# Two 64-row halves of experts side by side in TensorE's column groups, and the tail in token rows, in a hybrid encoder step on one core

## The chip, the cores and the metric

One Trainium2 chip, one of its cores. The metric is the device time of one execution in microseconds, the median of several runs; lower is better. Everything is float32.

## What is computed

One layer of a streaming encoder for 1024 prompt tokens and 8 sequences of 16 sample tokens, 1152 tokens of width 1024: RMSNorm, four mixer branches with gates, an output projection, then a second RMSNorm and a mixture of 16 experts, then a final RMSNorm. The change touches the experts and what is behind them:

```python
def _layer(...):
    ...
    h = _rmsnorm(x, P['norm_moe_w']) * (1.0 + sc_f) + sh_f
    f = _grouped_moe(h.reshape(bsz * L, D_MODEL), router_w, router_bias, ...)
    x = x + g_f * f.reshape(bsz, L, D_MODEL)

def _grouped_moe(h, router_w, router_bias, w_gate, w_up, w_down):
    ...
    def expert_block(args):
        xb, e = args
        return (jax.nn.silu(xb @ w_gate[e]) * (xb @ w_up[e])) @ w_down[e]
    yb = lax.map(expert_block, (buf.reshape(...), block_expert)).reshape(...)
    return jnp.zeros_like(h).at[t_s].add(yb[pos] * w_s[:, None])
```

The router picks two experts for every token, with weights. The width inside an expert is 512. g_f is one vector for all prompt tokens and one for each sample sequence. The 1152 tokens make 2304 rows, sorted by expert. On the reference's own inputs its router gives the 16 experts 102, 183, 150, 119, 126, 153, 182, 129, 163, 195, 169, 191, 79, 120, 128 and 115 rows. In blocks of 128 rows these fill 25 of the kernel's 33 blocks; in halves of 64 rows they fill 42 of 52. Blocks and halves behind the last one are given to expert 15 and computed too, since the program is the same for any routing.

## The kernel before

Five engines run their own instruction streams (blocks `nc.sync` or SP, which issues nearly all DMAs; `nc.tensor` or PE; `nc.scalar` or ACT; `nc.gpsimd` or POOL; `nc.vector` or DVE), each in the order written, and meet at hand-written semaphores.

The router's result goes through a stretch of small operations on DVE with transposes and small matmuls on PE, which gives for each block its expert and the token of each row. The normed tokens have been written to DRAM as rows (`h_rows`). Then come the blocks, 0 to 32. POOL gathers 128 rows into `xg`; PE turns them (`turn_block`, L1260, 8 transposes), ACT copies them to `xT`. PE multiplies them by the gate weights and by the up weights (L1291, 8 + 8 matmuls of 512 columns into banks 0 and 1), ACT and DVE form silu(gate) * up, PE turns that (L1301, 4 transposes), and multiplies it by the down weights (`down_block`, L1277, 8 matmuls). PE's order in block j is gate, up, turn of block j + 1, down of block j - 1, turn of the hidden rows of j.

An expert's weights are 6 MB: 2 MB gate, 2 MB up, 2 MB down. SBUF has room for two sets, and the blocks use them in turn by expert: the address comes from a register. SP's loop reads three numbers for block j from a table (`value_load`: expert of the next set, whether block j begins a new expert, and the address of the other set), and when block j begins a new expert it loads the expert after it into the other set (L826 gate and up, L829 down). An issue with `cond` false moves nothing. Then SP stores the output rows of block j - 1 to DRAM (L709).

The tail is three phases with barriers between them (`end_phase`). For each of 9 chunks of 128 tokens POOL gathers the two output rows of a token (L1683), DVE scales and adds them (L2239, L2240), PE turns the sum to feature layout (L1312), DVE multiplies by g_f (L2246) and adds x (L2250). Then the final RMSNorm over all tokens (squares on ACT, sums with a matrix of ones on PE, L510; the root on ACT; the reciprocal and the scaling on DVE, L530 and L2254), then one store of the whole output and three small ones.

## Time and profile before

| what | value |
|---|---|
| median of 3 runs | 3228.3 us (3225.89 to 3230.79) |
| the profiled execution, its time | 3229.76 us |
| its span, first to last instruction | 3227.6 us |
| mean granted TensorE clock | 0.943 |
| busy: PE, PEld, DVE, ACT, POOL | 2881.0, 1727.9, 1119.8, 673.8, 48.8 us |
| busy on L1291 (gate, up) and L1277 (down) | 461.5 and 232.2 us |

PE is the matmul stream and PEld the loading of its stationary operand, which runs beside it. A float32 matmul of the program is two MATMUL records in the trace, a transpose is one. Starts are what counts: the end of a record is modelled, and records of a full stream overlap. The granted clock is 1.0 for 2.4 GHz and 0.5 for 1.2 GHz. SPq is SP's queue of DMA issues.

### The profile page before, as it was taken

The numbers are of one execution on the slowest core, as the hardware profiler recorded it, in microseconds if no ns is written. First come the engines' busy times: TensorE is split into PE (matmuls) and PEld (weight loads), VectorE is DVE, ScalarE is ACT, GpSimd is POOL, SyncE is SP. The second block draws the span as 40 slices with busy tenths as digits, with TensorE's granted clock in tenths as the row PEclk, the third lists the DMA queues.
The fourth block names the chain that finished last, engine by engine and source line by source line (L and its number), as shares of the span: only waits on it lengthen the run. The fifth ranks groups of instructions, "written<-read, shape, count | busy, mean of one in ns | idle before, by whom it ended". The sixth has DMA issues, their size and how long they took to land. (4 is left out here: it accounts for less than half of the span.)

```text
span 3227.6 us, 27447 instructions
## 1 busy us (share of the span) xinstructions
PE 2881.0 (89%) x10827; PEld 1727.9 (54%) x10827; DVE 1119.8 (35%) x1718; ACT 673.8 (21%) x1144; POOL 48.8 (2%) x56
## 2 busy tenths in 40 slices
PE   6998999989899997898599998989879999999953
PEld 3556777765455665454355566655434444444422
DVE  5794444324232354331311567223430000000034
ACT  2442322212111111112200265311301011011001
POOL 0000000000000000000000000000000000000010
PEclk9999999979999998999799999999979999999976
DMA  6001121112010112110001101230165745573132
GB/s 260 27 26 58 41 89 65 37 37 111 26 52 26 41 49 107 56 53 26 26 26 39 40 24 48 96 134 6 59 257 192 271 172 196 202 278 133 40 107 95
DMA packets 41260, 292.73 MB, mean 91 GB/s; under 512 B 4528, under 2 KB 17200, under 8 KB 29872
## 3 DMA queue, kind: packets, MB, share of 16 engines
q1 hardware_dynamic: 33792, 264.24, 21.0%
q0 software_dynamic: 7344, 26.74, 2.5%
q8 instruction: 89, 1.46, 0.2%
q14 instruction: 35, 0.29, 0.0%
HBM read 345.52 MB, written 46.11 MB: 121 GB/s over the span
## 5 line engine op out<-in xcount | busy, mean ns | idle before, releaser
L492 PE MATMUL psum<-arena 128*128 128x384 f32 x3168 | 1037.7, 490 | 80.4 <-DVEq L318 61.8
L492 PEld LDWEIGHTS psum<-arena 128*128 128x128 f32 x3168 | 606.8, 192 | 509.1 <-DVEq L318 65.5
L1291 PE MATMUL psum<-arena 128*128 x1056 | 461.5, 595 | 1.9 <-ACT arena L1640 1.9
L652 PE MATMUL psum<-arena 128*128 128x384 f32 x1152 | 406.6, 497 | 16.8 <-DMA arena<-in_gate 14.3
L1291 PEld LDWEIGHTS psum<-arena 128*128 128x128 f32 x1056 | 199.1, 191 | 241.0 <-issue 241.0
L652 PEld LDWEIGHTS psum<-arena 128*128 128x128 f32 x1152 | 213.3, 194 | 138.1 <-DMA arena<-in_gate 15.2
L1277 PE MATMUL psum<-arena 128*128 x528 | 232.2, 592 | 1.1 <-DVE arena L2230 1.1
L2226 DVE TENSOR_TENSOR arena<-arena,psum 128x512 f32<-128x512 f32 x33 | 22.7, 688 | 437.3 <-issue 401.1
L1277 PEld LDWEIGHTS psum<-arena 128*128 128x128 f32 x528 | 97.8, 190 | 112.3 <-issue 112.3
L633 DVE TENSOR_TENSOR arena<-arena,psum 128x1152 f32<-128x1152 f32 x32 | 43.3, 1354 | 313.4 <-PE psum L492 313.4
L1176 PE MATMUL psum<-arena 128*128 128x384 f32 x384 | 127.8, 492 | 8.2 <-DMA arena<-in_out 8.2
L530 DVE RECIPROCAL arena<-arena 128x1152 f32<-128x1152 f32 x14 | 102.9, 7353 | 59.6 <-ACT arena L525 38.9
L1176 PEld LDWEIGHTS psum<-arena 128*128 128x128 f32 x384 | 72.9, 192 | 58.8 <-issue 11.4
L2220 DVE COPY arena<-psum 128x512 f32<-128x512 f32 x33 | 22.8, 691 | 230.4 <-PE psum L1277 230.4
L588 DVE SCALAR_TENSOR_TENSOR arena<-arena,vec 128x1024 f32<-128x1024 f32 x72 | 92.5, 1285 | 2.5
L1794 DVE TENSOR_TENSOR arena<-arena,psum 128x256 f32<-128x256 f32 x120 | 48.2, 421 | 120.9 <-PE psum L943 120.7
L931 PE MATMUL psum<-arena 128*128 128x128 f32 x480 | 76.0, 284 | 15.8 <-DVE arena L1794 12.0
L1640 ACT ACTIVATE arena<-psum 128x1024 f32<-128x1024 f32 x33 | 33.8, 1023 | 266.0 <-PE psum L1260 266.0
L557 ACT ACTIVATE arena<-hist 128x24 f32<-128x24 f32 x24 | 5.4, 226 | 349.7 <-PE psum L492 326.2
L931 PEld LDWEIGHTS psum<-arena 128*128 128x128 f32 x480 | 62.2, 191 | 29.0 <-issue 20.3
L665 ACT ACTIVATE arena<-psum 128x384 f32<-128x384 f32 x72 | 35.1, 490 | 200.1 <-PE psum L652 199.8
L510 PE MATMUL psum<-arena,cst 128*128 128x384 f32 x144 | 55.2, 536 | 23.7 <-ACT arena L518 23.7
(482 smaller groups left out, 2664.9 us busy)
## 6 DMA issues: line engine op xcount, KB each, us to landing
arena<-in_moe SPq DMA_DIRECT2D x33, 4096.0 KB
arena<-in_moe SPq DMA_DIRECT2D x33, 2048.0 KB
arena<-in_ada SPq DMA_DIRECT2D x12, 2048.0 KB, 9.0
y_rows<-arena SPq DMA_DIRECT2D x33, 512.0 KB, 2.9
arena<-in_gate SPq DMA_DIRECT2D x8, 2048.0 KB, 7.9
gate_raw<-arena SPq DMA_DIRECT2D x72, 192.0 KB, 1.8
arena<-gate_raw SPq DMA_DIRECT2D x6, 2304.0 KB, 9.2
arena<-in_br SPq DMA_DIRECT2D x4, 2048.0 KB, 9.7
```

The source lines that it names most:

```text
L492: last = nc.tensor.matmul(pset(s)[:, n, :], w[:, kk, :], src[:, kk, n * N3:(n + 1) * N3], start=(kk == 0), stop=(kk == K - 1))
L510: last = nc.tensor.matmul(pset(s)[:, n, :], ones, sq[q % 2][:, n * N3:(n + 1) * N3], start=(i == 0), stop=(i == len(terms) - 1))
L530: V.then(nc.vector.reciprocal(rs, rt), s_recip)
L588: nc.vector.scalar_tensor_tensor(out=dst[:, 0:NP_TOK], in0=a, scalar=w, in1=dst[:, 0:NP_TOK], op0=ALU.mult, op1=ALU.add)
L633: nc.vector.tensor_tensor(tri3(dst), tri3(sig), pset(s), ALU.mult).then_inc(s_free[s], 1)
L652: last = nc.tensor.matmul(bank(6 + u % 2)[:, 0:N3], w[:, m % 4, kk, :], HT[:, kk, n * N3:(n + 1) * N3], start=(kk == 0), stop=(kk == KD - 1))
L665: nc.scalar.activation(stage[k][u % 2], bank(6 + u % 2)[:, 0:N3], ACT.Copy).then_inc(g_ev, 1)
L931: last = nc.tensor.matmul(bank(5 * f)[:, hs[e]], cLK[lv % 2][:, hs[h]], gX[h], start=True, stop=True)
L1176: last = nc.tensor.matmul(bank(u % 4)[:, 0:N3], wo[m // 4][:, m % 4, k, :], merged[:, k, n * N3:(n + 1) * N3], start=(k == 0), stop=(k == ...
L1277: last = nc.tensor.matmul(bank(6 + n), ehT[:, k * P:(k + 1) * P], arena[:, bass.ds(at + (8192 + 1024 * k + 512 * n), 512)], start=(k == 0) ...
L1291: last = nc.tensor.matmul(bank(w), x[:, k * P:(k + 1) * P], arena[:, bass.ds(at + (4096 * w + 512 * k), 512)], start=(k == 0), stop=(k == ...
L1794: tt(x, x, bank(1 + f)[:, 0:256], ALU.subtract).then_inc(c_x, 1)
```

## The change

Experts. The unit is a half of 64 rows. The 52 halves stand in two lists of 26, and step j takes half j and half 26 + j: both are gathered as one tile of 128 rows. List i has a weight set of its own at a fixed address (`wset[i]`), and each matmul of before is now two, for 64 rows each, with the outputs in partitions 0 to 63 and 64 to 127 of one bank. There are 26 steps in place of 33 blocks. Since a list has one set, its three parts are overwritten in place: SP's loop waits until gate, up and down are through with the old weights and loads the new ones part by part (`load_part`), 2 MB each and each conditional. ACT now copies all 1024 columns of the result (`yr`), DVE multiplies them by the prompt's g_f (`yb`), and both are stored, to `y_raw` and `y_rows`.

Routing. The tables are fewer and the copying of g_f to rows is new: 10 small DMAs, one PE transpose. x is turned to token rows in place: 18 units of 4 transposes on PE (`x_rows`) and a copy on ACT, put between PE's waits for the routing.

Tail. It runs in token rows, without barriers between its parts: per chunk 4 gathered buffers ahead, two scaled additions on DVE, square with sum, root, reciprocal of 128 numbers, and the turn to feature layout as 8 matmuls with a diagonal matrix that holds the reciprocals, then scaled copies by half on DVE and on ACT, and a store for each chunk. The sample chunk takes its rows from `y_raw` and multiplies by its g_f. The three small output stores move ahead of the experts.

```diff
 KM = MIX // P
 GH, SH = 4, 8
 NE = 16
-BLK = 128
-NB = (2 * T + NE * (BLK - 1)) // BLK
+BLK = 64
+NBP = ((2 * T + NE * (BLK - 1)) // BLK + 1) // 2
+NB = 2 * NBP
 EPS = 1e-6
...
-        wset = cut(0, 12288)
+        wset = [cut(0, 12288), cut(WSET, 12288)]
...
+        yr = [cut(19968, D), cut(20992, D)]
+        gate_p, gate_s = cut(43520, D), cut(44544, D)
+        gate_t = cut(45568, P)[0:72]
+        yg = [[cut(WSET * (i >= 6) + 2048 * (i % 6) + 1024 * k, D) for k in range(2)] for i in range(NT)]
+        fdg = [cut(12288 + P * i, P) for i in range(2)]
+        fss, frt, frs = [small[:, 256 + 9 * i:256 + 9 * (i + 1)] for i in range(3)]
+        y_raw = nc.dram_tensor("y_raw", (NB * BLK, D), F32, kind="Internal").ap()
+        gate_rows = nc.dram_tensor("gate_rows", (72, P), F32, kind="Internal").ap()
...
         def store_block(sp, j):
 
             sp.wait_ge(e_ya, j + 1)
+            sp.dma_start(y_raw[j * P:(j + 1) * P, :], yr[j % 2]).then_inc(e_st[j % 2], 16)
             sp.wait_ge(e_yd, j + 1)
-            sp.dma_start(y_rows[j * BLK:(j + 1) * BLK, :], yb[j % 2]).then_inc(e_st[j % 2], 16)
+            sp.dma_start(y_rows[j * P:(j + 1) * P, :], yb[j % 2]).then_inc(e_st[j % 2], 16)
 
 
         @block.sync
...
+            def half_expert(j, i):
+
+                e = sp.value_load(eint[:, 0, NBP * i + j:NBP * i + j + 1], min_val=0, max_val=NE - 1)
+                return A["moe"][bass.ds(e, 1)].rearrange("a p c -> (a p) c")
+
+            first = [half_expert(0, i) for i in range(2)]
+            for i in range(2):
+                sp.dma_start(wset[i][:, 0:4096], first[i][:, 0:4096]).then_inc(e_wg, 16)
+            for i in range(2):
+                sp.dma_start(wset[i][:, 4096:8192], first[i][:, 4096:8192]).then_inc(e_wu, 16)
...
+            def load_part(j, a, b, done):
+
+                for i in range(2):
+                    new = sp.value_load(eint[:, 1, NBP * i + j:NBP * i + j + 1], min_val=0, max_val=1)
+                    sp.dma_start(wset[i][:, a:b], half_expert(j, i)[:, a:b], cond=(new > 0)).then_inc(done, 16)
+
+            for j in range(1, NBP + 1):
+                if j < NBP:
+                    sp.wait_ge(e_g, j)
+                    load_part(j, 0, 4096, e_wg)
                     sp.wait_ge(e_u, j)
-                sp.dma_start(arena[:, bass.ds(other, 8192)], expert[:, 0:8192], cond=(new > 0)).then_inc(e_w[j % 2], 16)
-                if j:
+                    load_part(j, 4096, 8192, e_wu)
                     sp.wait_ge(e_d, j)
-                sp.dma_start(arena[:, bass.ds(other + 8192, 4096)], expert[:, 8192:12288],
-                             cond=(new > 0)).then_inc(e_wd[j % 2], 16)
-                if j:
...
+                    load_part(j, 8192, 12288, e_wd)
+                store_block(sp, j - 1)
+            for s, c in enumerate(CHUNKS):
+                sp.wait_ge(f_e, s + 1)
+                sp.wait_ge(f_w, s + 1)
+                sp.dma_start(A["yT"][:, :, c * P:(c + 1) * P], hd(yg[s][1], 8)).then_inc(s_out, 16)
+            sp.wait_ge(s_out, 16 * (3 + NT))
...
+            def x_rows(v0, v1):
+
+                for v in range(v0, v1):
+                    c, u = v // 2, 2 * NT + 1 + v
+                    pe.wait_ge(m_htok, u - 1)
+                    for k in range(4):
+                        last = nc.tensor.transpose(bank(5 + u % 2)[:, P * k:P * (k + 1)],
+                                                   X[:, 4 * (v % 2) + k, c * P:(c + 1) * P], ident)
+                    last.then_inc(m_ht, 1)
...
+            def down_block(j):
+
+                pe.wait_ge(e_wd, 32 * (j + 1))
                 pe.wait_ge(e_htc, j + 1)
                 if j:
                     pe.wait_ge(e_ya, j)
-                    pe.wait_ge(e_yd, j)
                 for n in range(2):
                     for k in range(4):
-                        last = nc.tensor.matmul(bank(6 + n), ehT[:, k * P:(k + 1) * P],
-                                                arena[:, bass.ds(at + (8192 + 1024 * k + 512 * n), 512)],
-                                                start=(k == 0), stop=(k == 3))
+                        for i in range(2):
+                            o = 64 * i
+                            last = nc.tensor.matmul(bank(6 + n)[o:o + 64], ehT[:, k * P + o:k * P + o + 64],
+                                                    wset[i][:, 8192 + 1024 * k + 512 * n:8192 + 1024 * k + 512 * (n + 1)],
+                                                    start=(k == 0), stop=(k == 3))
                 last.then_inc(e_d, 1)
 
             turn_block(0)
...
+            for j in range(NBP):
                 pe.wait_ge(e_xc, j + 1)
                 x = xT[j % 2]
-                for w, s in ((0, e_g), (1, e_u)):
+                for w, ready, s in ((0, e_wg, e_g), (1, e_wu, e_u)):
+                    pe.wait_ge(ready, 32 * (j + 1))
                     for k in range(KD):
-                        last = nc.tensor.matmul(bank(w), x[:, k * P:(k + 1) * P],
-                                                arena[:, bass.ds(at + (4096 * w + 512 * k), 512)],
-                                                start=(k == 0), stop=(k == KD - 1))
+                        for i in range(2):
+                            o = 64 * i
+                            last = nc.tensor.matmul(bank(w)[o:o + 64], x[:, k * P + o:k * P + o + 64],
+                                                    wset[i][:, 4096 * w + 512 * k:4096 * w + 512 * (k + 1)],
+                                                    start=(k == 0), stop=(k == KD - 1))
                     last.then_inc(s, 1)
...
-                    down_block(j - 1, before)
+                    down_block(j - 1)
...
+            down_block(NBP - 1)
+            for s in range(NT):
+                pe.wait_ge(f_d, s + 1)
+                if s >= 4:
+                    pe.wait_ge(f_e, s - 3)
+                    pe.wait_ge(f_w, s - 3)
                 for k in range(KD):
-                    last = nc.tensor.transpose(bank(2 * (c % 2) + k // 4)[:, P * (k % 4):P * (k % 4 + 1)],
-                                               ff[c % 2][:, k * P:(k + 1) * P], ident)
+                    last = nc.tensor.matmul(bank(2 * (s % 4) + k // 4)[:, P * (k % 4):P * (k % 4 + 1)],
+                                            yg[s][0][:, k * P:(k + 1) * P], fdg[s % 2], start=True, stop=True)
                 last.then_inc(f_t, 1)
...
                 if j >= 2:
-                    act.wait_ge(e_st[j % 2], 16 * (j // 2))
-                nc.scalar.activation(yb[j % 2][:, 0:512], bank(6), ACT.Copy).then_inc(e_ya, 1)
+                    act.wait_ge(e_st[j % 2], 32 * (j // 2))
+                nc.scalar.activation(yr[j % 2], psum[:, 3072:4096], ACT.Copy).then_inc(e_ya, 1)
...
+            for s in range(NT + 2):
+                if 1 <= s < NT + 1:
+                    i = s - 1
+                    act.wait_ge(o_rs, UP_RS + i + 1)
+                    if i >= 2:
+                        act.wait_ge(f_t, i - 1)
+                    nc.scalar.activation(fdg[i % 2], ident, ACT.Identity, scale=frs[:, i:i + 1]).then_inc(f_d, 1)
+                if s >= 2:
+                    i = s - 2
+                    act.wait_ge(f_t, i + 1)
+                    for k in range(4, KD):
...
+                if s < NT:
+                    act.wait_ge(f_f, s + 1)
+                    S.then(nc.scalar.activation(yg[s][1], yg[s][0], ACT.Square, accum_out=fss[:, s:s + 1]))
+                    nc.scalar.activation(frt[:, s:s + 1], fss[:, s:s + 1], ACT.Sqrt, bias=c_("eps"),
+                                         scale=1.0 / D).then_inc(o_root, 1)
...
+            for i in range(2):
+                pool.wait_ge(e_st[i], 32 * ((NBP + 1 - i) // 2))
+            for s, c in enumerate(CHUNKS):
+                if s >= 4:
+                    pool.wait_ge(f_f, s - 3)
                 for k in range(2):
-                    pool.indirect_dma_start(out=yg[c % 2][k], out_offset=None, in_=y_rows,
+                    pool.indirect_dma_start(out=yg[s][k], out_offset=None, in_=y_raw if c == NT - 1 else y_rows,
                                             in_offset=bass.IndirectOffsetOnAxis(
-                                                ap=posi[:, NT * k + c:NT * k + c + 1], axis=0)).then_inc(f_y[c % 2], 16)
+                                                ap=posi[:, NT * k + c:NT * k + c + 1], axis=0)).then_inc(f_y[s % 4], 16)
...
+            dve_down(NBP - 1)
+            for s in range(NT + 2):
+                if s < NT:
+                    c = CHUNKS[s]
+                    y0, y1 = yg[s]
+                    xc = X[:, :, c * P:(c + 1) * P]
+                    dve.wait_ge(f_y[s % 4], 32 * (s // 4 + 1))
+                    if c < NT - 1:
+                        V.then(stt(out=hd(y0, 8), in0=hd(y0, 8), scalar=w12[:, 0, c:c + 1], in1=xc, op0=ALU.mult, op1=ALU.add))
+                    else:
+                        V.then(ts(y0, y0, w12[:, 0, c:c + 1], None, ALU.mult))
+                if 1 <= s < NT + 1:
+                    i = s - 1
+                    dve.wait_ge(o_root, UP_ROOT + i + 1)
+                    V.then(nc.vector.reciprocal(frs[:, i:i + 1], frt[:, i:i + 1]), o_rs)
+                if s < NT:
+                    if c < NT - 1:
+                        V.then(stt(out=y0, in0=y1, scalar=w12[:, 1, c:c + 1], in1=y0, op0=ALU.mult, op1=ALU.add), f_f)
+                    else:
+                        V.then(stt(out=y0, in0=y1, scalar=w12[:, 1, c:c + 1], in1=y0, op0=ALU.mult, op1=ALU.add))
+                        V.then(tt(y0, y0, gate_s, ALU.mult))
+                        V.then(tt(hd(y0, 8), hd(y0, 8), xc, ALU.add), f_f)
+                if s >= 2:
+                    i = s - 2
+                    dve.wait_ge(f_t, i + 1)
+                    tt(hd(yg[i][1][:, 0:512], 4), hd(bank(2 * (i % 4)), 4), over(v_("norm_final", 0, 4), P),
```

In the diff of the DVE part the copy of the result becomes:

```diff
             def dve_down(j):
-                dve.wait_ge(e_d, j + 1)
-                if j >= 2:
-                    dve.wait_ge(e_st[j % 2], 16 * (j // 2))
-                nc.vector.tensor_copy(yb[j % 2][:, 512:1024], bank(7)).then_inc(e_yd, 1)
-            for j in range(NB):
+                dve.wait_ge(e_ya, j + 1)
+                tt(yb[j % 2], yr[j % 2], gate_p, ALU.mult).then_inc(e_yd, 1)
+            dve.wait_ge(m_grow, 16 * (2 + NSEQ))
+            for j in range(NBP):
                 dve.wait_ge(e_sg, j + 1)
                 dve.wait_ge(e_u, j + 1)
```

What the change does to the order on SP, in the steady part of the loop. Before, from the wait for down (`e_d`) to the next gate and up load, whose weights are for a later expert:

```order
L829 ISA [waits e_d]
L829 REGISTER_ALU
L829 DMA arena<-in_moe 128x4096
L709 DMA y_rows<-arena 128x1024 [waits e_yd,e_ya]
L820 TENSOR_LOAD hist
L820 ISA x2
L821 TENSOR_LOAD hist
L821 ISA x2
L822 TENSOR_LOAD hist
L822 ISA x2
L826 ISA [waits e_u]
L826 REGISTER_ALU
```

Now, from the second set's part of down to the first set's part of gate of the next step. Ahead of these rows stands the same group of six for the first set, which begins with the wait for `e_d`; behind them stands the group of the second set's gate part:

```order
L846 TENSOR_LOAD hist
L846 ISA x2
L823 TENSOR_LOAD hist
L823 ISA x2
L847 ISA
L847 DMA arena<-in_moe 128x4096
L710 DMA y_raw<-arena 128x1024 [waits e_ya]
L712 DMA y_rows<-arena 128x1024 [waits e_yd]
L846 TENSOR_LOAD hist [waits e_g]
L846 ISA x2
L823 TENSOR_LOAD hist
L823 ISA x2
```

One load with three numbers ahead of it has become two loads with two numbers each, and the gate part that the next step reads now stands behind the wait for down and behind both stores.

On PE, a step now. The rows of L1327 are gate and up, L1299 the turn of the next rows, L1313 down of the step before, L1337 the turn of the hidden rows:

```order
L1327 MATMUL psum<-arena 64x512 [waits e_wg,e_xc]
L1327 MATMUL psum<-arena 64x512 x15
L1327 MATMUL psum<-arena 64x512 [waits e_wu]
L1327 MATMUL psum<-arena 64x512 x15
L1299 MATMUL psum<-cst,arena 128x128 [waits e_xc,e_x1]
L1299 MATMUL psum<-cst,arena 128x128 x7
L1313 MATMUL psum<-arena 64x512 [waits e_ya,e_htc,e_wd]
L1313 MATMUL psum<-arena 64x512 x15
L1337 MATMUL psum<-cst,arena 128x128 [waits e_hid]
L1337 MATMUL psum<-cst,arena 128x128 x3
```

Gate and up have a wait for their own weights (`e_wg`, `e_wu`) in every step, each count of which comes from SP's row L847 of that same step, and there are twice as many matmuls of half the rows.

## Rows read from the trace of the kernel before

**Rows 1.** The page's first line.

```profile
span 3227.6 us, 27447 instructions
```

**Rows 2.** Blocks and tail: stretch, length, busy PE, PEld, DVE, ACT, POOL, clock, DMA.

```profile
2371.90:3102.90 731.00, 727.92 (x1980) 342.86 (x1980) 64.63 (x98) 73.86 (x99) 29.03 (x31) 0.99 0.48 184
3102.90:3227.60 124.70, 35.37 (x120) 24.09 (x120) 59.77 (x46) 12.29 (x11) 16.85 (x18) 0.59 0.34 122
```

**Rows 3.** Timeline of PE and ACT in the last blocks: start, length, line.

```profile
3065.29 1.04 PE L1260 MATMUL psum<-cst,arena 128*128 128x128 f32 x8
3066.16 7.03 PE L1277 MATMUL psum<-arena 128*128 x16
3066.36 1.02 ACT L1640 ACTIVATE arena<-psum 128x1024 f32<-128x1024 f32 x1 [7.14 <-PE psum L1260]
3073.03 0.60 PE L1301 MATMUL psum<-cst,arena 128*128 128x128 f32 x4
3073.47 13.90 PE L1291 MATMUL psum<-arena 128*128 x32
3087.21 7.03 PE L1277 MATMUL psum<-arena 128*128 x16
```

**Rows 4.** Timeline of PE where 64-column operands alternate between partition halves.

```profile
1090.03 0.44 PE L1055 MATMUL psum<-arena 128*64 128x128 f32 x4
1090.25 0.44 PE L1057 MATMUL psum<-arena 128*64 128x128 f32 x4
1091.12 0.44 PE L1057 MATMUL psum<-arena 128*64 128x128 f32 x4
1091.49 1.13 PE L1071 MATMUL psum<-arena 128*128 128x256 f32 x4
```

**Rows 5.** Timeline of SP's issues in two blocks, then the L821 loads' durations.

```profile
2481.86 0.09 SPq L829 DMA_DIRECT2D arena<-in_moe  x1
2482.30 0.35 SPq L709 DMA_DIRECT2D y_rows<-arena  x1
2485.34 0.35 SPq L826 DMA_DIRECT2D arena<-in_moe  x1
...
2504.23 0.36 SPq L709 DMA_DIRECT2D y_rows<-arena  x1
2506.72 0.34 SPq L826 DMA_DIRECT2D arena<-in_moe  x1
...
L821 SPq TENSOR_LOAD <-hist x32: 261/290/855, 2370.4 to 3053.1; - x32
```

**Rows 6.** A 2 MB load alone (to landing), and 6 MB of expert weights.

```profile
arena<-in_gate SPq DMA_DIRECT2D x8, 2048.0 KB, 7.9
...
2352.39:2369.84 17.45, 7.86 (x36) 7.75 (x36) 11.95 (x29) 0.00 (x0) 2.50 (x2) 0.50 0.92 368
```

**Rows 7.** An idle stretch of PE, and stretches right behind idle ones.

```profile
257.40:266.20 8.80, 0.05 (x2) 0.04 (x1) 5.75 (x10) 3.69 (x6) 0.00 (x0) 0.70 0.63 238
266.20:274.50 8.30, 8.30 (x39) 8.30 (x40) 2.86 (x6) 2.51 (x4) 0.00 (x0) 0.50 0.00 1
1774.10:1779.80 5.70, 5.70 (x9) 3.16 (x10) 4.62 (x26) 0.19 (x2) 0.00 (x0) 0.50 0.62 267
1847.00:1851.50 4.50, 4.48 (x7) 2.52 (x8) 0.00 (x0) 4.44 (x12) 0.00 (x0) 0.50 0.00 0
2169.30:2172.30 3.00, 2.98 (x5) 1.79 (x6) 0.00 (x0) 0.00 (x0) 0.00 (x0) 0.50 1.06 401
```

**Rows 8.** The tail: costliest groups of PE and DVE, then two rows of its timeline.

```profile
L1312 PE MATMUL psum<-cst,arena 128*128 128x128 f32 x72 | 17.7, 427 | 50.8 <-DVE arena L2240 50.8
L2240 DVE SCALAR_TENSOR_TENSOR arena<-arena,hist 128x1024 f32<-128x1024 f32 x9 | 11.6, 1284 | 0.3
...
3106.58 0.94 POOL L1683 DMA_INDIRECT arena<-y_rows,hist  x1 [82.87 <-ACTq L318]
3113.38 0.75 DVE L2239 TENSOR_SCALAR arena<-arena,hist 128x1024 f32<-128x1024 f32 x1 [9.76 <-DMA arena<-y_rows,hist]
```

203 lines of the change are left out of this document (71 added, 132 removed).

## The prediction

> **What bounds the kernel now.** I read the stretches first, then the timeline of PE, then that of SP. The span is 3227.6 us [rows 1]. The change leaves everything before the router alone, so two stretches matter: the expert blocks, 731.0 us, in which PE is busy for 727.9, and the tail, 124.7 us, in which PE is busy for 35.4 and DVE for 59.8 [rows 2]. In the blocks the reader is to see a chain of PE work without a hole: turn 0.87 us (3065.29 to 3066.16), down 6.87 (to 3073.03), turn of the hidden rows 0.44 (to 3073.47), gate and up 13.74 (to 3087.21), 21.92 together [rows 3]. Weights never hold it up, since they come for the next expert, into the other set. The tail is bound by waits between engines, not by any of them.
>
> **Streams side by side.** The new step has twice the matmuls of half the rows. What two of them cost together is shown by four-record groups whose results go in turn to partitions 0 to 63 and 64 to 127: they start 0.22 us apart (1090.03, 1090.25), 0.055 for a record of 128 columns [rows 4], where 8 records one after the other take 0.87, 0.109 each [rows 3]. So two column groups run at once and a pair costs one. I take 13.74 and 6.87 us for the pairs. Going back to the full form, the next record starts 0.37 after the last group (1091.12 to 1091.49) in place of 0.22 [rows 4]: 0.15 a switch, four in a step, 0.6 (bounds 0 and 0.6). A step of pure PE work is then 21.92 + 0.6 = 22.5 us, and 26 in place of 33 would save about 140. A rule of the Trainium skill speaks against the full pairing: TensorE: Matmul & The Clock Gate, Measured speedup vs the span model, gives 2.38 times for three column tiles of 512 columns, which is 0.79 of the ideal. By it a pair would cost 1.26 of one, 5.4 us more in a step and some 140 us more in all; the trace has 1.98 times for two.
>
> **The wait that is put in.** This is the large term. Gate of step j + 1 needs `e_wg`, whose count is given by SP in every step, whether it loads or not, and these issues now stand behind the wait for down of step j - 1, behind the down parts and behind both stores. PE has only the turn of the hidden rows left when down ends. I count from there. SP's 13 instructions before (three register loads of three instructions, three for the address, of which the order doesn't print a move, and the issue) take 3.04 us less the store's 0.35 in one block and 2.49 less 0.36 in the other, plus 0.09 for an issue that moves nothing: 2.78 and 2.22, mean 2.5 [rows 5]. That two values exist is seen in L821, 0.26 to 0.86 us for the same load. A set's part now is 9 such instructions (two register loads, address, move, issue): 2.5 x 9/13 = 1.73. Four of them (down and gate, two sets each) are 6.9; the two stores are 0.44 each (2481.86 to 2482.30) [rows 5], 0.9; for the semaphores at both ends I take 0.2. Sum 8.0 us, bounds 7.2 (all loads short) and 9.0 (all long). Whether an issue that moves nothing raises its semaphore at once no row says: at least 0, at most the 7.9 of a real 2 MB load [rows 6]; I take 0, as no packet is sent. The copy on ACT (1.02 [rows 3]) and the multiplication on DVE (at most 1.28 [rows 8]) end 2.5 us after down and lie beside the down parts; without that cover they would add 2.5. Of the 8.0, 0.4 is covered by the turn of the hidden rows, so a steady step is 22.5 - 0.4 + 8.0 = 30.1 us. In the first step SP is not yet behind down, so 24 of the 25 transitions have it. Queued behind the wait on PE is all the rest of the step, and the loads of up follow gate's at once, covered by gate's 6.9 us.
>
> **The clock.** PE now stands idle some 7.5 us in each step. Before, an idle stretch of 8.80 us had a clock of 0.70 in the mean, and the work right behind was at 0.5 for 8.3 us; behind three others it was 5.7, 4.5 and 3.0 us [rows 7]. Work at 1.2 GHz loses half its time: 4.1, 2.9, 2.2, 1.5. I take 2.5 a step (bounds 1.5 and 4.1).
>
> **Loads that move something.** They are in place, so their whole length shows. The router's counts make 42 halves: list 0 changes its expert at steps 2, 5, 8, 10, 12, 15, 18, 21, 24, list 1 at 2, 5, 8, 10, 12, 14. So five steps load both sets, five load one. 2 MB take 7.9 us from issue to landing, and 6 MB 17.45 (370 GB/s), so 4.8 for each further 2 MB [rows 6]. The first issue comes 1.5 us after the stores. Both sets: 1.5 + 7.9 + 4.8 = 14.2, less the 3.5 which the two parts take anyway, 10.7 us more. One set: 9.4 - 3.5 = 5.9, or 7.6 where it is the second. Up's 2 MB parts land 4.8 apart behind gate's, within gate's 6.9 plus the slow clock. Down's have a whole step. Together 5 x 10.7 + 4 x 5.9 + 7.6, and 4 for the issues of real down parts: 89 us (bounds 60, if they overlap the steady wait better, and 120, with the gathers in the same queues).
>
> **Sum of the expert stretch.** From its start: 3.3 to the first gate; the first step 13.7 + 0.9 + 0.4, 1 for the silu, 2.5 clock, 18.5; 24 transitions of 30.1 + 2.5 = 32.6, 782; the last step and its own down 13.7 + 6.9 + 0.4 + 1.1 + 6.9 + 0.6, 29.6; loads 89. 923 us in place of 731.0, 192 more.
>
> **Routing stretch.** 18 units of 4 transposes enter PE's waits for DVE. Eight transposes take 0.87 [rows 3], so they cost 8 us, 16 at 1.2 GHz, if that cover were gone. DVE has less to compute, SP ten small DMAs more, ahead of a table that it needs only after the first gate. I take 0, bounds -3 and +5.
>
> **Tail.** Up to the first gather 5.4 us: copy 1.0, multiplication 1.3, store and its landing 3.1 as now (before 3.7 in all). First gather to DVE 6.8 (3106.58 to 3113.38) [rows 8]. Then per chunk DVE has two 1.28 [rows 8], about 0.6 for half a copy and 0.3 for the rest, 3.5; PE has 16 records in place of 8 that took 1.97 at the low clock (17.7/9) [rows 8], 3.9 at most. 9 chunks by 3.5 to 3.9 and 2 for the sample chunk: 35. Drain of the pipeline and the last store: 11. Sum 58 in place of 124.7. What goes is the 50.8 us of PE waits on L2240 and the final norm's three passes. I take -65, bounds -50 and -72.
>
> **Sum.** 192 - 65 = +127 us on a profiled execution of 3227.6 (its time was 3229.76, the median of the runs 3228.3, 1.5 lower). On the median this gives 3355; as the real loads may hide a little of the clock's loss (the ten longest waits have one ramp, too) I round down to 3350.
>
> **Rivals.**
> - *SP's chain is short* (faster side). If a part costs 0.8 us and not 1.73, the chain is 4.3 us, the idle time under 4, and the clock may stay up: 24 x (3.7 + 2.5) = 149 less, 3201. The chain decides below about 5 us, if the clock holds with it. For it speaks the 0.09 us of an idle issue; against it both rows of SP, where three loads never took under 2 us. Chance 0.05.
> - *Pairs overlap only in part.* 512 columns in two groups may not stream as 128 do. If a pair costs a quarter more than one: 26 x 5.2 = 134 more, 3484; with no overlap at all 26 x 20.6 more, 3886. Against it stands [rows 4]. The 1.26 of the Trainium skill (TensorE: Matmul & The Clock Gate, as above) would give 3490. Chance 0.05.
> - *The loads cost more than I count*: weights, gathers and two stores in the same queues, up parts late too, so that each of the ten load steps costs 8 us more and the steady wait is at its upper bound: +80 + 24, 3450. For it: 4 MB of gate, 4 of up and 1 of stores are issued within 9 us, and 9 MB at 370 GB/s take 24 us. Chance 0.12.
> - *No change*: the wait costs what the smaller number of steps and the tail give, 3228. It needs 5 us less in each transition. Chance 0.02.
> - *The wait is smaller, near both lower bounds* (7.2, clock 1.5, loads 60): 3355 - 19 - 24 - 29 = 3283. Chance 0.08.
> - My forecast, 3295 to 3405: 0.68.
>
> **How the numbers follow.** The likeliest case gives 3350. Adding its bounds as independent (chain 20, clock 30, loads 30, tail 10, switches 10) gives about 50 each way; to leave no more than 2 in 10 out the range goes from 3290 to 3410. The measurement tells 0.2% from no change. Slower by over 0.2%: all but the first and the fourth case, 0.93; within 0.02; faster 0.05.
>
> **What would show it.** In the changed kernel's trace: L1327 records in pairs, 0.43 us or less from pair to pair at the high clock (right), 0.5 or more (the second rival). PE idle before gate in nearly every step, 7 to 8 us, ended by the gate weights' semaphore, on SP a chain of register loads between down and the gate issue. Ten waits of 13 to 19 us. A clock of 0.5 at the head of each gate. Expert stretch about 920 us, tail about 60. The forecast falls if the steady wait is under 5 us, or if the clock stays at 1.0 through it.

## The result, and the profile after

The changed kernel takes 3366.4 us (median of 4 runs, 3364.0 to 3369.2), the kernel before in the same call 3228.3 (4 runs): ratio 1.043, 95% interval 1.041 to 1.045. It is slower by 138 us. The forecast was 3350, range 3290 to 3410. Each profile is one execution.

The page of the changed kernel, its first line, and two of its costliest groups (busy us, mean ns | idle just before, and what ended most of it):

```profile
span 3364.0 us, 29126 instructions
...
L1327 PE MATMUL psum<-arena 128*64 128x512 f32 x1664 | 415.8, 662 | 281.8 <-DMA arena<-in_moe 280.1
...
L1313 PE MATMUL psum<-arena 128*64 128x512 f32 x832 | 184.2, 595 | 2.5 <-DMA arena<-in_moe 2.5
```

Stretches of the changed kernel: the expert steps from the first turn on, then the tail (us, busy PE, PEld, DVE, ACT, POOL, clock, share and GB/s of the DMA engines). They answer to [rows 2].

```profile
2382.98:3308.10 925.12, 640.75 (x2808) 231.04 (x2808) 64.23 (x77) 69.05 (x78) 22.44 (x24) 0.84 0.39 149
3308.10:3364.00 55.90, 22.85 (x146) 21.02 (x144) 33.74 (x39) 27.63 (x74) 21.68 (x18) 0.76 0.80 272
```

The reader is to see that PE works less than before in the expert steps, 641 us in place of 728 [rows 2], and that the steps still take 194 us more: 282 us of idle time stand ahead of the gate and up records, nearly all ended by weights. The tail takes 69 us less. That is 125, and the first turn comes 11 us later: 136, the difference of the two spans.

One step without loads, PE's timeline and then SP's (start, length, engine, line; in brackets the idle time and what ended it):

```profile
2502.94 0.66 PE L1337 MATMUL psum<-cst,arena 128*128 128x128 f32 x4
2511.44 15.28 PE L1327 MATMUL psum<-arena 128*64 128x512 f32 x64 [7.84 <-DMA arena<-in_moe]
2526.65 1.09 PE L1299 MATMUL psum<-cst,arena 128*128 128x128 f32 x8
2527.67 7.09 PE L1313 MATMUL psum<-arena 128*64 128x512 f32 x32
```

```profile
2504.50 1.64 SPq L847 DMA_DIRECT2D arena<-in_moe  x2
2506.18 0.34 SPq L710 DMA_DIRECT2D y_raw<-arena  x1
2506.57 0.43 SPq L712 DMA_DIRECT2D y_rows<-arena  x1
2509.66 4.83 SPq L847 DMA_DIRECT2D arena<-in_moe  x4
```

Nothing is loaded in this step. PE has turned the hidden rows and waits 7.84 us. Meanwhile SP reads its registers and issues two empty down parts (the first at 2504.50), then the stores, reads again, and issues the two empty gate parts (the first at 2509.66, the second 1.58 later). PE starts 0.2 us behind that second one, so an issue that moves nothing raises its semaphore within 0.2 us.

### The profile page after: what moved, and what is told of

Read it like the earlier page. It is cut to its first block, busy times and chain, and to the rows that moved or that the text cites. A ratio compares the mean times of both kernels' runs of the same rounds, so it can differ in the third digit from the quotient of the medians.

```text
span 3364.0 us, 29126 instructions
## 1 busy us (share of the span) xinstructions
PE 2796.6 (83%) x11752; PEld 1624.3 (48%) x11752; DVE 1088.4 (32%) x1680; ACT 695.2 (21%) x1205; POOL 46.6 (1%) x49
## 4 chain that ended last, share of the span: by engine, by line
PE 73%; DVE 9%; DMA 6%; SPq 5%; ACT 3%; issue 3%; POOL 0%; DVEq 0%; ACTq 0%; POOLq 0%
PE psum L492 31%; PE psum L1327 12%; PE psum L654 8%; PE psum L1313 5%; PE psum L1199 4%; DMA arena<-in_moe 3%; PE psum L954 2%; SPq L823 2%; SPq L846 2%; SPq L847 1%; PE psum L510 1%; PE psum L943 1%; PE psum L966 1%; PE psum L1299 1%; DVE arena L1847 1%
## 5 line engine op out<-in xcount | busy, mean ns | idle before, releaser
L492 PEld LDWEIGHTS psum<-arena 128*128 128x128 f32 x3168 | 608.1, 192 | 510.9 <-DVEq L319 65.5
L1327 PE MATMUL psum<-arena 128*64 128x512 f32 x1664 | 415.8, 662 | 281.8 <-DMA arena<-in_moe 280.1
L1327 PEld LDWEIGHTS psum<-arena 128*64 128x64 f32 x1664 | 139.5, 153 | 541.6 <-issue 533.8
L654 PEld LDWEIGHTS psum<-arena 128*128 128x128 f32 x1152 | 213.2, 194 | 138.1 <-DMA arena<-in_gate 15.3
L1313 PE MATMUL psum<-arena 128*64 128x512 f32 x832 | 184.2, 595 | 2.5 <-DMA arena<-in_moe 2.5
L1690 ACT ACTIVATE arena<-psum 128x512 f32<-128x512 f32 x26 | 15.5, 597 | 503.3 <-PE psum L1327 503.3
L1313 PEld LDWEIGHTS psum<-arena 128*64 128x64 f32 x832 | 57.7, 137 | 111.1 <-issue 108.3
L530 DVE RECIPROCAL arena<-arena 128x1152 f32<-128x1152 f32 x13 | 95.6, 7353 | 39.1 <-ACT arena L525 38.9
L2257 DVE TENSOR_TENSOR arena<-arena 128x1024 f32<-128x1024 f32 x26 | 31.9, 1225 | 216.2 <-ACT arena L1684 216.2
L1199 PEld LDWEIGHTS psum<-arena 128*128 128x128 f32 x384 | 72.9, 192 | 58.7 <-issue 11.4
L954 PEld LDWEIGHTS psum<-arena 128*128 128x128 f32 x480 | 62.2, 191 | 29.0 <-issue 20.2
L1421 ACT ACTIVATE arena<-psum 128x256 f32<-128x256 f32 x120 | 46.1, 384 | 125.2 <-PE psum L954 124.3
```

Of the source, the lines that this page charges most:

```text
L492: last = nc.tensor.matmul(pset(s)[:, n, :], w[:, kk, :], src[:, kk, n * N3:(n + 1) * N3], start=(kk == 0), stop=(kk == K - 1))
L530: V.then(nc.vector.reciprocal(rs, rt), s_recip)
L654: last = nc.tensor.matmul(bank(6 + u % 2)[:, 0:N3], w[:, m % 4, kk, :], HT[:, kk, n * N3:(n + 1) * N3], start=(kk == 0), stop=(kk == KD - 1))
L954: last = nc.tensor.matmul(bank(5 * f)[:, hs[e]], cLK[lv % 2][:, hs[h]], gX[h], start=True, stop=True)
L1199: last = nc.tensor.matmul(bank(u % 4)[:, 0:N3], wo[m // 4][:, m % 4, k, :], merged[:, k, n * N3:(n + 1) * N3], start=(k == 0), stop=(k == ...
L1313: last = nc.tensor.matmul(bank(6 + n)[o:o + 64], ehT[:, k * P + o:k * P + o + 64], wset[i][:, 8192 + 1024 * k + 512 * n:8192 + 1024 * k + ...
```

## Experiments

### Early issue: gate and up parts ahead of the wait for down

```diff
-            for j in range(1, NBP + 1):
+            for j in range(1, NBP + 2):
                 if j < NBP:
                     sp.wait_ge(e_g, j)
                     load_part(j, 0, 4096, e_wg)
                     sp.wait_ge(e_u, j)
                     load_part(j, 4096, 8192, e_wu)
-                    sp.wait_ge(e_d, j)
-                    load_part(j, 8192, 12288, e_wd)
-                store_block(sp, j - 1)
+                if 2 <= j <= NBP:
+                    sp.wait_ge(e_d, j - 1)
+                    load_part(j - 1, 8192, 12288, e_wd)
+                if j >= 2:
+                    store_block(sp, j - 2)
```

PE does down of step j - 1 behind up of step j. The change waits for the count `e_d` >= j, that is for down of step j - 1, before it comes to the next gate part. Here that wait stands behind the gate and up parts of the next step, whose own conditions (`e_g`, `e_u`) are met long before.

> One edit: SP asks for gate and up of step j+1 as soon as gate and up of step j are through, ahead of the wait for down; the down part and the stores of a step keep their place behind down. My theory (the slowdown is the chain of SP instructions behind the wait for down, plus the clock and the loads that show behind it): the idle time ahead of gate, 280 us in the changed kernel, goes nearly all, the slow clock at the head of gate with it (51 us), and both-set loads leave 1 to 3 us in front of up in five steps. Span 3364 - 280 - 51 + 10 = 3043, a ratio to the kernel before of 0.943. Rival, the queues' bandwidth: the five steps that load both sets move 12.6 MB at some 370 GB/s, 34 us against a step of 22, so 12 us a step stay, 60 in all, and 3100. Second rival, pairs cost more than one: no change beyond the idle time, but steps of more than 23 us.

Measured: 3068.7 us (3066.7 to 3069.2), ratio to before 0.950 (0.948 to 0.951). It beats both kernels. PE's timeline of two steps:

```profile
2888.53 13.95 PE L1329 MATMUL psum<-arena 128*64 128x512 f32 x64
2902.42 1.09 PE L1301 MATMUL psum<-cst,arena 128*128 128x128 f32 x8
2903.44 7.09 PE L1315 MATMUL psum<-arena 128*64 128x512 f32 x32
2910.46 0.66 PE L1339 MATMUL psum<-cst,arena 128*128 128x128 f32 x4
2911.05 13.95 PE L1329 MATMUL psum<-arena 128*64 128x512 f32 x64
```

There is no hole, and the step is 22.52 us (2888.53 to 2911.05), the 22.5 of the forecast. From the first gate the expert steps take 627.6 us in place of 922.0. The order of the waits on SP thus accounts for the loss: with it go the idle time, the slow clock behind it and most of what the loads cost. The span is 3066.6 us, 24 more than the theory's 3043. That miss lies in the steps that load both sets, for which the theory had 10 us and the rival 60. By the distances of the gate starts in this trace the five of them, each with the steps next to it, add 3.6, 7.3, 6.6, 9.3 and 9.1 us to the plain ones, 36 in all. The single loads cost 0.2 us together. 12 MB of weights at the 370 GB/s of [rows 6] take 34 us, more than the step has.

### Only the gate part ahead of the down part

```diff
+            sp.wait_ge(e_g, 1)
+            load_part(1, 0, 4096, e_wg)
             for j in range(1, NBP + 1):
                 if j < NBP:
-                    sp.wait_ge(e_g, j)
-                    load_part(j, 0, 4096, e_wg)
                     sp.wait_ge(e_u, j)
                     load_part(j, 4096, 8192, e_wu)
                     sp.wait_ge(e_d, j)
+                    if j + 1 < NBP:
+                        load_part(j + 1, 0, 4096, e_wg)
                     load_part(j, 8192, 12288, e_wd)
                 store_block(sp, j - 1)
```

> One edit: behind the wait for down SP asks for the next gate part first, then for the down part, then stores. The wait for down stays. My theory: the chain in front of gate is 3.8 us in place of 8.6, 4.8 less in 24 transitions (115 us); up's part now ends about a microsecond after gate, 24 us back; idle time of 3.3 us leaves the clock up, another 51 us. Span about 3222; if the clock falls all the same, 3273. Rival (the wait is something that ends with down itself, as a semaphore or the stores): no gain, 3364.

Measured: 3268.6 us, one execution. PE's timeline of one step:

```profile
2937.64 0.66 PE L1339 MATMUL psum<-cst,arena 128*128 128x128 f32 x4
2940.92 7.09 PE L1329 MATMUL psum<-arena 128*64 128x512 f32 x32 [2.63 <-DMA arena<-in_moe]
2949.53 7.09 PE L1329 MATMUL psum<-arena 128*64 128x512 f32 x32 [1.52 <-DMA arena<-in_moe]
```

The wait ahead of gate falls from 7.84 to 2.63 us, since only the two gate parts are left in it. The second wait, ahead of up, was expected too, with 1 us a step: the up part now stands behind the down parts and the stores. Here it is 1.5 us; over the 14 steps without loads its mean is 0.7, since a slow gate hides it. So a step without loads behind another one is 6.1 us shorter than in the changed kernel, where 5.9 were expected. What was missed is in the steps with loads. Where both sets are loaded, up waits 3.5 to 4.0 us for its weights, and the stretch from the gate of a load step to the next gate is only 1.2 us shorter in the mean. That makes 43 of the 50 us by which the expert steps fall short (92 us gained from the first gate on, 142 expected).

After the wait ahead of gate the clock held in 8 of the 14 steps without loads (first to 32nd gate record 6.50 us) and fell in 6 (8.15 to 8.19): in three of eleven behind waits of 2.6 to 2.7 us, and in all three behind 3.0.

### The pause filled with matmuls

```diff
                 last.then_inc(e_ht, 1)
+                if 1 <= j < NBP - 1:
+                    if j == 1:
+                        pe.wait_ge(m_htok, 4 * NT + 1)
+                    for k in range(8):
+                        nc.tensor.matmul(bank(5), ident, c_("level", 0, 512), start=True, stop=True)
             down_block(NBP - 1)
```

> Eight more matmuls of 512 columns (identity times a constant, 6.9 us, into a bank that nobody reads) behind the turn of the hidden rows in steps 1 to 24, inside PE's wait. It prices the clock alone. My theory: the 14 steady transitions lose 2.15 us each to the slow clock at the head of gate; that goes, 30 us less, 3334; in the ten load steps PE still idles 5 us or more behind the extra work and nothing changes there. Rival (gate starts slowly for another reason, its weights just landed or the change of form): 3364 or a little more, and gates as long as now.

Measured: 3335.9 us, one execution, 30.5 less than the change. One step of it, and two stretches (the pause, then gate):

```profile
2673.82 7.03 PE L1343 MATMUL psum<-cst 128*128 128x512 f32 x16
2681.29 13.96 PE L1327 MATMUL psum<-arena 128*64 128x512 f32 x64 [0.44 <-DMA arena<-in_moe]
```

```profile
2673.82:2681.29 7.47, 7.04 (x18) 2.89 (x17) 1.82 (x2) 0.65 (x1) 0.00 (x0) 1.00 0.73 279
2681.29:2688.20 6.91, 6.91 (x33) 2.81 (x35) 0.00 (x0) 0.00 (x0) 0.00 (x0) 1.00 0.98 350
```

With the pause filled, gate runs at a clock of 1.00 and takes 6.9 us, in 13 of the 14 plain steps, and the wait itself is as long as before: a plain step is 30.4 us (32.7 without the extra matmuls, next experiment), so 2.3 of it are the clock. In the steps with loads, whose wait is longer than the filling, the clock falls all the same; that is why 30 us come back and not the 50 that all 24 gates lose.

### No weights moved behind the first

```diff
-            V.then(tt(erow[:, 1, 1:NB], erow[:, 0, 1:NB], erow[:, 0, 0:NB - 1], ALU.not_equal))
+            V.then(tt(erow[:, 1, 1:NB], erow[:, 0, 1:NB], erow[:, 0, 1:NB], ALU.not_equal))
```

All steps compute with the first two experts' weights; each conditional load is issued and moves nothing.

> The table entry for a new expert is always 0: every conditional issue stays, none moves data, and all steps use the two first experts' weights (so the experts' output is another one). My theory: the ten load steps fall to the steady 32.8 us, 83 us less, 3281, and the rest stays as it is. Rival (the steady wait is really the queue working through stores and gathers): the steady steps get shorter too, below 3250.

Measured: 3274.8 us, one execution, 91.5 less than the change. Its expert steps, from the first gate:

```profile
2380.40:3216.31 835.91, 642.11 (x2800) 230.67 (x2800) 64.21 (x77) 67.95 (x77) 21.54 (x24) 0.87 0.14 51
```

835.9 in place of 922.0, so the loads cost 86 us (forecast 89). The 23 periods from the gate of step 2 to that of step 25 have a mean of 32.7 us (forecast 32.6).

### The two column groups apart

On the early-issue kernel, gate and up; down the same way:

```diff
-                    for k in range(KD):
-                        for i in range(2):
+                    for i in range(2):
+                        for k in range(KD):
                             o = 64 * i
```

> This is the early-issue kernel (3068.7 us) with one thing changed: in gate, up and down all matmuls of column group 0 come first, then all of column group 1, instead of taking turns. Work, weights and waits are the same. Theory: two groups overlap only where their records stand side by side in the order, so a step's 20.6 us of pairs become 41.2, 26 x 20.6 = 536 more, about 3600 us less what the loads' waits (about 40) then hide: 3565 to 3610. Rival (overlap does not depend on the order, or the step was bound by something else than the matmul stream): 3068, no change. If something between comes out, pairs overlap across a distance.

Measured: 3307.0 us (3305.4 to 3308.6, 2 runs), ratio to before 1.024 (1.022 to 1.026), 238 us more than with the groups in turns: between the two. Gate and up of one step in the timeline, then the records of L1329 in 4.6 us at the head of gate by the view of the line, here and in the early-issue kernel:

```profile
2937.57 22.70 PE L1329 MATMUL psum<-arena 128*64 128x512 f32 x64
```

```profile
L1329 PE MATMUL psum<-arena x12: 592/592/643, 2937.6 to 2942.3; 128*64 128x512 f32 x12
```

```profile
L1329 PE MATMUL psum<-arena x24: 592/592/643, 2911.0 to 2915.8; 128*64 128x512 f32 x24
```

12 records in the one, 24 in the other: in turns, two streams run; one group alone starts a record each 0.43 us. So it is the order that pairs them. But the first record of the second group starts when the 13th of the 16 of the first does (5.21 and 5.20 us into gate): the last four of a group run beside the first four of the other. That saves 4 x 0.43 = 1.7 us at a seam, and a step has six (three in gate and up, three in down), 10.3 us in all. So the step grows by 10.6 us, from 22.5 to 33.1, and not by 20.6. In this trace every step from the second on takes 33.1, those with loads too: the longer step hides them all, which gives back the 36 us, and 26 x 10.6 - 36 is the 240 that the times show.

### The first gather ahead of the weights

On the early-issue kernel: of the first two experts only the gate weights are issued ahead of the first gather.

```diff
-            for i in range(2):
-                sp.dma_start(wset[i][:, 4096:8192], first[i][:, 4096:8192]).then_inc(e_wu, 16)
-            sp.wait_ge(m_ht, 2 * NT)
-            sp.dma_start(wset[0][:, 8192:12288], first[0][:, 8192:12288]).then_inc(e_wd, 16)
             sp.wait_ge(m_grow, 16)
...
-            sp.wait_ge(m_route, ROUTE_IDX)
-            sp.dma_start(wset[1][:, 8192:12288], first[1][:, 8192:12288]).then_inc(e_wd, 16)
+            sp.wait_ge(e_x[0], 16)
+            for i in range(2):
+                sp.dma_start(wset[i][:, 4096:8192], first[i][:, 4096:8192]).then_inc(e_wu, 16)
+            for i in range(2):
+                sp.dma_start(wset[i][:, 8192:12288], first[i][:, 8192:12288]).then_inc(e_wd, 16)
             sp.wait_ge(m_route, ROUTE_TAB)
```

> This is the early-issue kernel (3068.7 us) with one thing changed: of the first two experts only the gate weights (4 MB) are issued ahead of the first gather; up and down (8 MB) are issued when that gather has landed. Theory (in the changed kernel the first gather queued behind the weights: 13.4 us from the table of rows to the first turn, 6.9 before): the first turn comes about 5 us earlier, and up's weights may be 1 to 2 us late for the first up; 4 us less in all, 3065, at most 6 less. Rival (the gather's own time, or the gate weights alone, set it): the first turn where it was, then up's weights late by several us: 3070 to 3075.

Measured: 3065.1 us (3064.1 to 3070.4, 5 runs), ratio to before 0.949 (0.948 to 0.951). In time it can't be told from the early-issue kernel, whose interval overlaps it. The trace shows the mechanism. First the kernel before, then the changed kernel, then this one: the cast of the first table of rows, and the first turn.

```profile
2365.06 0.20 DVE L2204 CAST hist<-psum 128x33 int32<-128x33 f32 x1 [4.52 <-PE psum L1251]
2371.93 1.94 PE L1260 MATMUL psum<-cst,arena 128*128 128x128 f32 x8 [6.98 <-DMA arena<-h_rows,hist]
```

```profile
2369.63 0.18 DVE L2252 CAST hist<-psum 128x26 int32<-128x26 f32 x1 [6.27 <-PE psum L1290]
2382.98 1.97 PE L1299 MATMUL psum<-cst,arena 128*128 128x128 f32 x8 [8.94 <-DMA arena<-h_rows,hist]
```

```profile
2365.47 0.18 DVE L2253 CAST hist<-psum 128x26 int32<-128x26 f32 x1 [6.27 <-PE psum L1291]
2372.74 1.36 PE L1300 MATMUL psum<-cst,arena 128*128 128x128 f32 x8 [2.85 <-DMA arena<-h_rows,hist]
```

13.35 us from the table to the turn in the changed kernel, 7.27 here; the kernel before had 6.9. Nearly all of the 6 us is given back: up of the first step waits 1.8 us for its weights, and the steps that load both sets, counted as above, add 40 us in this trace in place of 36. Why these add more no run tells.

### SP's register reads ahead of the wait

On the changed kernel, with its order of waits, issues and stores kept:

```diff
+            def read_part(j):
+
+                return [(sp.value_load(eint[:, 1, NBP * i + j:NBP * i + j + 1], min_val=0, max_val=1),
+                         half_expert(j, i)) for i in range(2)]
...
+            part = read_part(1)
             for j in range(1, NBP + 1):
                 if j < NBP:
                     sp.wait_ge(e_g, j)
-                    load_part(j, 0, 4096, e_wg)
+                    load_part(part, 0, 4096, e_wg)
                     sp.wait_ge(e_u, j)
-                    load_part(j, 4096, 8192, e_wu)
+                    load_part(part, 4096, 8192, e_wu)
+                    ahead = read_part(j + 1) if j + 1 < NBP else None
                     sp.wait_ge(e_d, j)
-                    load_part(j, 8192, 12288, e_wd)
+                    load_part(part, 8192, 12288, e_wd)
+                    part = ahead
                 store_block(sp, j - 1)
```

> This is the changed kernel (3366.4 us) with its order of waits, issues and stores kept; only SP's register reads (expert and whether to load, for both sets) are done once a step, ahead of the wait for down, instead of inside each part behind it. Behind the wait for down stand four conditional issues and two stores. Theory (the register reads are what makes the 8.6 us wait): what stays is the copy on ACT 1.05, the multiplication on DVE 1.3, the store's issue 0.45, two issues 0.3 and the semaphores 0.4, about 3.5 us of wait; 24 x 5.1 = 122 less; and if the clock stays up after the shorter pause, 24 x 2.1 = 50 more off: 3195 to 3245. Rival (the order is what costs: a round trip over stores and issues, whatever the reads take): the wait stays above 6 us, 3310 or more.

Measured: 3266.5 us (3265.2 to 3269.7, 4 runs), ratio to before 1.012 (1.010 to 1.013). 100 us less than the change, but short of the expected 121 to 171. SP's issues and PE's gate of one plain step, and the pause and gate as stretches:

```profile
2656.96 0.95 SPq L851 DMA_DIRECT2D arena<-in_moe  x2
2657.96 0.42 SPq L710 DMA_DIRECT2D y_raw<-arena  x1
2659.02 0.33 SPq L712 DMA_DIRECT2D y_rows<-arena  x1
...
2660.64 15.61 PE L1334 MATMUL psum<-arena 128*64 128x512 f32 x64 [3.40 <-DMA arena<-in_moe]
```

```profile
2657.20:2660.64 3.44, 0.05 (x1) 0.03 (x1) 1.83 (x2) 0.53 (x1) 0.00 (x0) 0.99 0.80 267
2660.64:2669.20 8.56, 8.55 (x32) 2.97 (x34) 0.00 (x0) 0.00 (x0) 0.00 (x0) 0.80 1.00 383
```

The steady wait is what was expected, 3.4 us here and 3.0 in ten of the 14 plain steps, and now the copy and the multiplication set it: the second store is issued at 2659.02, behind DVE's multiplication, 1.1 us behind the first. Two terms missed. The clock still fell: the pause had 0.99 and gate behind it 0.80, 8.6 us in place of 6.9. It fell in all 14 plain steps (first to 32nd gate record 8.0 to 9.2 us in place of 6.5), which take 27.3 us where the one before is plain too. And in the steps with loads less came back (double loads 38.7 to 40.8 us in place of 41.2 to 44.4, in the mean 2.7 less), since there the transfer is what is waited for.

### The same, with the shorter pause filled

Four extra matmuls in the same place as above.

> This is the changed kernel with the register reads ahead (3266.5 us) and four extra matmuls of 512 columns (identity times a constant, into a bank that nothing reads) behind the turn of the hidden rows in steps 1 to 24, which fill 3.5 of the 3.8 us that PE waits there. Theory (even after a pause of 3.8 us the gate records run slower, 8.19 us in place of 6.49 from the first to the 32nd, because the clock has gone down): in the 14 steps without a load they take 6.5, 24 us less, and a little in the others: 3240 (3234 to 3246). Rival (the gate records are slow for another reason, the operands or the weights' arrival): 3266, no change or some us more.

Measured: 3247.7 us (3244.1 to 3253.8, 4 runs), ratio to before 1.006 (1.004 to 1.008).

```profile
2652.53 3.60 PE L1350 MATMUL psum<-cst 128*128 128x512 f32 x8
2656.09 13.95 PE L1334 MATMUL psum<-arena 128*64 128x512 f32 x64
```

18.8 us less, somewhat short of the theory's 20 to 32. The plain steps are 25.95 us in place of 27.3, their gates 6.9: the slow gate was the clock. The clock gives back 1.7 us a step; the filling is 0.3 us longer than the wait that it fills.

### Early issue, gather first and reads ahead

> This is the kernel with the first gather ahead of the weights and early issue (about 3065 us) with the register reads done once a step ahead of the waits as well. Theory (what is left over in the expert stretch, about 35 us, is in the five steps that load both sets and is counted from the first gate issue: 12 MB at 370 GB/s take 34 us): the first issue of such a step comes 1.5 us sooner and the second set's 3.2 us, so each of the five steps gains 2 to 3 us: 3050 to 3056. Rival (these steps are bound by what the queues carry in all, gathers and stores with them, from an earlier moment): no more than 2 us less than the other, 3063 to 3066.

The same `read_part`, in the early-issue loop. Measured: 3058.1 us (3049.9 to 3063.7, 5 runs), ratio to before 0.947 (0.945 to 0.948). It is the fastest of all. The kernel to compare it with is the one with the first gather ahead (3065.1 us). In its trace the double-load steps and those right behind them add 28 us to the plain ones, where they add 40 in the other: 2.4 for each of the five, as the theory had it (2 to 3). The time is 7 us less, between the theory and the rival. The runs of this kernel spread by 14 us (3049.9 to 3063.7); they all lie below those of the other (3064.1 to 3070.4), but the intervals of the two ratios touch.

### One chunk's gathers at a time in the tail

On that kernel:

```diff
-                if s >= 4:
-                    pool.wait_ge(f_f, s - 3)
+                if s >= 1:
+                    pool.wait_ge(f_f, s)
```

> This is the early-issue kernel with the first gather ahead and the register reads ahead (3058.1 us) with one thing changed, in the tail: the gathers of a chunk are issued only when the chunk before is added, in place of up to four chunks ahead. Theory (in the tail DVE's work sets the pace, 3.4 us a chunk, since the rows are fetched ahead): a chunk now takes a gather to its landing, 6.4 us from issue to DVE's first row in the changed kernel's trace, plus the two additions, 2.6 us, some 9.3 in all, 5.9 more for each of eight: 47 us, 3105 (3095 to 3115). Rival (the tail is bound by the output stores or by ACT and PE, and would take the time anyway): 3058 to 3070.

Measured: 3111.5 us (3108.7 to 3116.9, 4 runs), ratio to before 0.963 (0.962 to 0.965). 53 us more, where 47 were expected. The tail as a stretch here, and then DVE's waits for the rows in the timeline:

```profile
3003.30:3114.70 111.40, 32.41 (x146) 30.12 (x144) 33.95 (x39) 27.62 (x74) 16.85 (x18) 0.59 0.44 137
```

```profile
3047.60 1.28 DVE L2284 SCALAR_TENSOR_TENSOR arena<-arena,hist 128x1024 f32<-128x1024 f32 x1 [7.12 <-DMA arena<-y_rows,hist]
3058.42 1.28 DVE L2284 SCALAR_TENSOR_TENSOR arena<-arena,hist 128x1024 f32<-128x1024 f32 x1 [7.29 <-DMA arena<-y_rows,hist]
```

10.8 us a chunk (9.3 expected). The tail is 111.4 us in place of the changed kernel's 55.9. So 55 of the 69 us that the new tail gains hang on the gathers issued ahead. The other 14 are then the rest of the change in the tail, by this subtraction only. The rival, that stores or ACT and PE set the pace, is out.

## Why the prediction was right

The mechanism and nearly all sizes were right. By its own steps:

- **Pairs cost one.** 0.43 us from pair to pair, a step of 22.51 with no wait in the early-issue kernel (22.5 forecast, four switches at 0.15 included: from start to start its four parts take 13.89, 1.02, 7.02 and 0.59, each 0.15 more than before). The order experiment shows that this hangs on taking turns. The 2.38 times of the Trainium skill (TensorE: Matmul & The Clock Gate, Measured speedup vs the span model), given for three column tiles and carried over to two as an estimate, would have made a pair 1.26 of one; the trace has two streams of 512 columns at full speed, 13.36 us from the first to the last of 64 records.
- **The wait on SP.** Forecast 8.0 us from the end of down, less 0.4 that the turn covers. Measured 7.84 of idle PE by the row above, and 7.9 more in the period of a filled step (30.4) than in one without the wait (22.5); the forecast had 7.6. A part of nine instructions takes 1.6 us behind another part, and 2.7 right behind the stores. Another order takes the wait away, and reads ahead of it take away more than half, so both are shown as its cause.
- **The clock.** 2.5 us a step forecast, 2.1 measured as the mean loss of the 24 gates, and 2.3 by the filled pause.
- **The loads.** 89 us forecast, 86 measured.
- **The tail.** -65 forecast (58 us), measured -69 (55.9 us).
- **Expert steps in sum.** 923 us forecast, 925.1 measured. That it fits to 2 us is in part luck: the wait was 0.3 us a step longer than forecast, the clock's loss 0.4 smaller and the loads 3 us smaller.
- **The routing stretch** is where the sum failed, by 11 us with a forecast of 0 and an upper bound of 5. What it named, the 18 units of x's rows and the ten small DMAs, add 0.7 us, with all else that is new in the routing (below). What it did not name: 8 MB of gate and up weights and 2 MB of down, and not 6 MB, are issued ahead of the first gather, which lands 6.5 us later; with 4 MB ahead of it, it lands as early as before. The other 4.6 us are there before the cast, and 3.9 of them before 2166.6 us, where the two programs have not yet issued one different instruction (the first is the store of `out_hist_out` on SP, 2173.44). The last DVE instruction ahead of that in both traces:

```profile
2162.64 1.36 DVE L639 TENSOR_TENSOR arena<-arena 128x1152 f32<-128x1152 f32 x1
```

```profile
2166.56 1.36 DVE L641 TENSOR_TENSOR arena<-arena 128x1152 f32<-128x1152 f32 x1
```

From there to the cast it is 202.4 us before and 203.1 now, so 0.7 is left for the change, 7.2 with the late gather, and the 3.9 are a difference between executions. In the traces of the seven experiments that leave the first loads as they are (the first five and the two with reads ahead in the changed kernel's order) the cast starts at 2363.9 to 2367.8, on both sides of the 2365.1 of the kernel before.

- **The rounding** from 3355 down to 3350 had no ground: the loads do not hide the clock's loss.

None of the rivals came true. Their places were tested one by one: SP's chain was not short, pairs overlap, the loads cost what was counted. A faster kernel, which the first rival had for another reason, came by edit: with the order changed the step falls to 22.5 us, and the kernel is 5% faster than before.

## What to carry to other kernels

A loop that issues its loads in one queue makes every issue wait for the condition of the issue before it, and a conditional load that moves nothing still holds the semaphore back that long. Put issues in the order in which their conditions come true, and read the registers of a dynamic load before the wait, not behind it. When a change saves work on the engine that sets the pace, add up what the issuing queue does between the last release and the first need: here a gain of 140 us met 8 us of it in each of 24 steps, which with the slow clock behind and the loads in place cost more than twice as much.

## What the runs showed of the hardware

- Two 64-column groups that take turns run side by side at full rate with 512 columns each (24 records in 4.6 us, 12 when one group runs alone), and in a block order they still overlap for four records at the seam (1.7 us).
- Behind idle stretches of PE of 2.6 to 3.0 us (the second experiment) gate ran at full clock in 8 plain steps of 14; behind 3.0 to 3.4 us (reads ahead) in none of 14; behind 7.8 to 8.2 us (no weights moved) in none of 24. The mean loss was 1.7 us behind the 3.0 to 3.4 and 2.1 behind the 7.8 to 8.2, so it grows far less than the pause.
- A register read on SP takes 0.27 us, but mostly 0.85 right behind the stores: 47 of the 48 reads for the first issue behind them in the kernel that moves no weights, 28 of 48 in the changed kernel. The rows are the second reads (L823) of one plain step of the kernel that moves no weights; first those of the down parts, then those behind the two stores, where one of two is slow:

```profile
L823 SPq TENSOR_LOAD <-hist x2: 269/270/270, 2652.2 to 2653.8; - x2
...
L823 SPq TENSOR_LOAD <-hist x2: 263/565/867, 2656.8 to 2659.0; - x2
```

Why, no run here tells.
